# A fp32 decoder layer on TensorE: moving rows stored as even tokens, then odd tokens, and read from both halves in turns

## The reference

```
proj = rmsnorm(x) @ w_in          # q, k, v, r, a_lr, conv (3), chunk-MLP (2)
out  = concat[GLA(q,k,v,a), ShortConv, ChunkMLP] @ w_out
h    = x + out
y    = h + (silu(n @ w_gate) * (n @ w_up)) @ w_down,   n = rmsnorm(h), width 5632
y    = rmsnorm(y)
```

## Time and profile before

| | |
|---|---|
| median of 3 runs | 2201.98 us (2200.2 to 2202.89) |
| profiled execution, span from first to last instruction | 2202.0 us |
| instructions | 41269 |
| busy share of the span: TensorE, DVE, ACT | 99%, 78%, 46% |
| matmuls | 17357 |
| HBM read, written | 267.09 MB, 56.63 MB |

### The profile page before, as it was taken

One profiled execution on the slowest core, in us unless ns is written; L12 is line 12 of the kernel. 1 busy time (PEld: TensorE's weight loads), 2 busy tenths in 40 slices (PEclk: granted clock), 3 DMA queues, 4 the chain that ended last, 5 costly groups with the idle time before them and its releaser, 6 DMA issues.

```text
span 2202.0 us, 41269 instructions
## 1 busy us (share of the span) xinstructions
PE 2189.9 (99%) x17357; PEld 2181.0 (99%) x17357; DVE 1710.5 (78%) x1987; ACT 1002.5 (46%) x1331; POOL 9.6 (0%) x15
## 2 busy tenths in 40 slices
PE   9999999999999999999999999999999999999998
PEld 9999999999999999999999999999999999999998
DVE  7765378546796789888887887888888888787887
ACT  7433523224454554444444544444444545444455
POOL 0000000000000000000000000000000000000000
PEclk9999999999999999999999999999999999999998
DMA  5332224245333435445445445444545876555523
GB/s 189 96 107 85 96 72 148 81 126 188 127 105 103 156 104 170 128 143 164 140 132 165 140 131 155 153 129 141 165 140 166 301 280 223 183 205 190 187 81 117
DMA packets 121516, 325.51 MB, mean 148 GB/s; under 512 B 10699, under 2 KB 51211, under 8 KB 120364
## 3 DMA queue, kind: packets, MB, share of 16 engines
q1 hardware_dynamic: 120860, 323.69, 44.0%
q10 hardware_dynamic: 528, 0.07, 0.0%
HBM read 267.09 MB, written 56.63 MB: 147 GB/s over the span
## 4 chain that ended last, share of the span: by engine, by line
PE 93%; DVE 3%; issue 1%; ACT 1%; DMA 1%; POOL 0%; POOLq 0%; DVEq 0%; ACTq 0%; SPq 0%
PE acc L1613 36%; PE g L1613 27%; PE acc L1300 18%; PE acc L1524 2%; PE g L1524 2%; PE acc L1562 2%; PE g L1562 1%; PE acc L1516 1%; PE g L1516 1%; DMA w_raw<-w_in 1%; DVE w_lo L2178 0%; PE g L1327 0%; PE g L1450 0%; DVE kd L2040 0%; PE g L1457 0%
## 5 line engine op out<-in xcount | busy, mean ns | idle before, releaser
L1121 ACT CAST w_hi<-w_s 128x1024 fp32r<-128x1024 f32 (+1 forms) x204 | 209.6, 1027 | 358.6 <-DVE w_s L2407 350.7
L1613 PE MATMUL acc<-op_hi,w_hi 128*128 128x272 f32 x1056 | 305.8, 290 | 0.3 <-ACT acc L1095 0.3
L1613 PE MATMUL acc<-sg_hi,w_hi 128*128 128x272 f32 x1056 | 305.9, 290 | 0.0
L1613 PE MATMUL g<-op_hi,w_hi 128*128 128x272 f32 x1056 | 305.8, 290 | 0.0
L1613 PE MATMUL acc<-op_hi,w_lo 128*128 128x272 f32 x1056 | 305.6, 289 | 0.0
L1613 PE MATMUL g<-op_hi,w_lo 128*128 128x272 f32 x1056 | 305.6, 289 | 0.0
L1613 PE MATMUL acc<-sg_hi,w_lo 128*128 128x272 f32 x1056 | 305.6, 289 | 0.0
L1613 PE MATMUL acc<-sg_lo,w_hi 128*128 128x272 f32 x1056 | 304.0, 288 | 0.0
L1613 PE MATMUL g<-op_lo,w_hi 128*128 128x272 f32 x1056 | 304.0, 288 | 0.0
L1613 PE MATMUL acc<-op_lo,w_hi 128*128 128x272 f32 x1056 | 304.0, 288 | 0.0
L1300 PE MATMUL acc<-op_hi,w_hi 128*128 128x272 f32 x1280 | 269.3, 292 | 0.0
(11 more groups left out here) (390 smaller groups left out, 5004.0 us busy)
## 6 DMA issues: line engine op xcount, KB each, us to landing
w<-w_gu SPq DMA_DIRECT2D x88, 512.0 KB, 3.3
w_raw<-w_gu SPq DMA_DIRECT2D x88, 512.0 KB, 4.1
w_raw<-w_in SPq DMA_DIRECT2D x64, 512.0 KB, 3.5
hf_dram<-hf_hi SPq DMA_DIRECT2D x22, 952.0 KB, 6.6
hf_dram<-hf_lo SPq DMA_DIRECT2D x22, 952.0 KB, 8.8
w_raw<-w_d SPq DMA_DIRECT2D x32, 512.0 KB, 4.4
w<-w_d SPq DMA_DIRECT2D x26, 512.0 KB, 3.3
op_hi<-hf_dram SPq DMA_DIRECT2D x16, 544.0 KB, 7.0
```

The source lines that it names most:

```text
L1121: nc.scalar.copy(w_hi[:, (C_ST + n) % RING, 0:w], src[:, 0:w]).then_inc(hi_ready, 1)
L1613: last = nc.tensor.matmul(out, w, x, start=fresh and j == 0 and i == 0, stop=j == h - 1 and i == 2, skip_group_check=True)
```

## The change

Within each half of 272 tokens, every activation row that a projection moves is stored as 136 even tokens followed by 136 odd tokens. The matmul's moving access names 136 pairs, the inner step of a pair being 136 elements (544 bytes), so it reads token 0 from the first half, token 1 from the second, token 2 from the first, and so on. Tokens enter the array, and PSUM, in their natural order.

The input comes a second time, as `xP`, in the new order on the host side; `load_x` reads it, while the residual is loaded from `xT` as before. Passes that make rows out of PSUM results or natural-order tiles read every second element and write runs. `mix_single_hi` becomes three copies, one per form. `var1` sums squares of the permuted input, so it reads in turns too. The diff, cut to its core (the same edit of the matmul stands at L1327, L1516, L1524 and L1562):

```diff
+        def turns(ap):
+            return ap.rearrange("p (a b) -> p b a", a=2)
+        def pairs(ap):
+            return ap.rearrange("p (b a) -> p b a", a=2)
+        def split2(ap):
+            return ap.rearrange("p (h b a) -> p h a b", h=ap.shape[1] // TH, a=2)
+        def halves(ap):
+            return ap.rearrange("p (h a b) -> p h a b", h=ap.shape[1] // TH, a=2)
+        def split_rows(ap):
+            return ap.rearrange("p i (b a) -> p i a b", a=2)
+        def half_rows(ap):
+            return ap.rearrange("p i (a b) -> p i a b", a=2)
...
-                sp.dma_start(trunk[:, 2 * i:2 * i + 2, :], xT[:, 2 * i:2 * i + 2, :]).then_inc(x_in[i], 16)
+                sp.dma_start(trunk[:, 2 * i:2 * i + 2, :], xP[:, 2 * i:2 * i + 2, :]).then_inc(x_in[i], 16)
...
-                nc.scalar.copy(op_hi[:, k, :], mix[:, MIX_ORDER[k], :]).then_inc(op_h, 1)
+                nc.scalar.copy(halves(op_hi[:, k, :]), split2(mix[:, MIX_ORDER[k], :])).then_inc(op_h, 1)
...
-                nc.scalar.copy(fa_hi[:, 0], mg[:, :, 0, :])
-                nc.scalar.copy(fa_hi[:, 1:3], mg[:, :, 2:4, :].rearrange("p i b t -> p b i t")).then_inc(fa_h, 1)
+                for f, b in enumerate((0, 2, 3)):
+                    last = nc.scalar.copy(half_rows(fa_hi[:, f]), split_rows(mg[:, :, b, :]))
+                last.then_inc(fa_h, 1)
...
-                nc.scalar.copy(ta_hi[f], mg[:, :, T_OF[f], :]).then_inc(ta_h, 1)
+                nc.scalar.copy(half_rows(ta_hi[f]), split_rows(mg[:, :, T_OF[f], :])).then_inc(ta_h, 1)
...
-                nc.scalar.mul(trunk[:, m, :], hst[:, m % 4, :], vec[:, V_G2 + m:V_G2 + m + 1]).then_inc(xg_done, 1)
+                nc.scalar.mul(halves(trunk[:, m, :]), split2(hst[:, m % 4, :]), vec[:, V_G2 + m:V_G2 + m + 1]).then_inc(xg_done, 1)
...
-                        last = nc.tensor.matmul(acc[t % 2][:, a, 0:TH], w, x[:, k, a * TH:(a + 1) * TH],
+                        last = nc.tensor.matmul(pairs(acc[t % 2][:, a, 0:TH]), w, turns(x[:, k, a * TH:(a + 1) * TH]),
...
-                    last = ones_product(g01, rstd[:])
+                    last = ones_product(g01, rstd[:], turns, pairs)
...
-                            last = nc.tensor.matmul(out, w, x, start=fresh and j == 0 and i == 0,
+                            last = nc.tensor.matmul(pairs(out), w, turns(x), start=fresh and j == 0 and i == 0,
...
-                nc.vector.tensor_tensor(ta_lo[f], mg[:, :, T_OF[f], :], f32(ta_hi[f]), ALU.subtract).then_inc(ta_rdy, 1)
+                nc.vector.tensor_tensor(half_rows(ta_lo[f]), split_rows(mg[:, :, T_OF[f], :]), half_rows(f32(ta_hi[f])), ALU.subtract)\
+                    .then_inc(ta_rdy, 1)
...
-                nc.vector.tensor_tensor(op_lo[:, k, :], mix[:, MIX_ORDER[k], :], f32(op_hi[:, k, :]), ALU.subtract)\
+                nc.vector.tensor_tensor(halves(op_lo[:, k, :]), split2(mix[:, MIX_ORDER[k], :]), halves(f32(op_hi[:, k, :])), ALU.subtract)\
...
-                nc.vector.tensor_tensor(hid[:, 2 * (q % 2):2 * (q % 2) + 2, :], two(gate),
-                                        two(up), ALU.mult).then_inc(hid_done, 1)
+                nc.vector.tensor_tensor(half_rows(hid[:, 2 * (q % 2):2 * (q % 2) + 2, :]), split2(gate),
+                                        split2(up), ALU.mult).then_inc(hid_done, 1)
...
+        "xP": feature_major(x).reshape(P, KT, 2, TH // 2, 2).transpose(0, 1, 2, 4, 3).reshape(P, KT, T),
```

More of the change, by code:

```diff
@@ L136, in up, with build @@
         return self.n
-def build(nc, xT, w_alr, w_in, w_kv, w_kc, w_oa, w_out, w_gu, w_d4, w_d3, vecs, wa2, wm, wsbd, bs, s0, cbuf, ident, tri, maskA, maskS,
+def build(nc, xT, xP, w_alr, w_in, w_kv, w_kc, w_oa, w_out, w_gu, w_d4, w_d3, vecs, wa2, wm, wsbd, bs, s0, cbuf, ident, tri, maskA, maskS,
           bmask, yT, gla_p, gla_s, conv_o, cmv):
@@ L1326, in alr_products @@
                     for a in range(2):
-                        mm = nc.tensor.matmul(g23[:, a, 0:TH], alw[:, k, :], x[:, k, a * TH:(a + 1) * TH],
+                        mm = nc.tensor.matmul(pairs(g23[:, a, 0:TH]), alw[:, k, :], turns(x[:, k, a * TH:(a + 1) * TH]),
                                               start=(k == 0 and n == 0), stop=(k == KT - 1 and n == 1))
@@ L1344, in _, with ones_product @@
                     mm.then_inc(chunk_done, 1)
-            def ones_product(out2, buf):
+            def ones_product(out2, buf, order=lambda ap: ap, out_order=lambda ap: ap):
                 for a in range(2):
-                    last = nc.tensor.matmul(out2[:, a, 0:TH], onesf[:], buf[:, a * TH:(a + 1) * TH],
+                    last = nc.tensor.matmul(out_order(out2[:, a, 0:TH]), onesf[:], order(buf[:, a * TH:(a + 1) * TH]),
                                             start=True, stop=True)
@@ L1515, in kv_product @@
                             for i, (w, x) in enumerate(((w_h, x_h), (w_h, x_l), (w_l, x_h))):
-                                last = nc.tensor.matmul(bank[:, side, 0:TH], w, x, start=False,
+                                last = nc.tensor.matmul(pairs(bank[:, side, 0:TH]), w, turns(x), start=False,
                                                         stop=j == KT - 2 * HQ - 1 and i == 2, skip_group_check=True)
@@ L1523, in kv_product @@
                     for i, (w, x) in enumerate(((w_h, x_h), (w_h, x_l), (w_l, x_h))):
-                        last = nc.tensor.matmul(banks[idx][:, side, 0:TH], w, x, start=idx < 2 and j == 0 and i == 0,
+                        last = nc.tensor.matmul(pairs(banks[idx][:, side, 0:TH]), w, turns(x), start=idx < 2 and j == 0 and i == 0,
                                                 stop=j == HQ - 1 and i == 2, skip_group_check=True)
@@ L1561, in mix_product @@
                         for i, (w, x) in enumerate(((w_h, x_h), (w_h, x_l), (w_l, x_h))):
-                            last = nc.tensor.matmul(out, w, x, start=idx < 2 and j == 0 and i == 0,
+                            last = nc.tensor.matmul(pairs(out), w, turns(x), start=idx < 2 and j == 0 and i == 0,
                                                     stop=j == HP - 1 and i == 2, skip_group_check=True)
@@ L2201, in mix_forms @@
                 dve.wait_ge(fa_h, 1)
-                nc.vector.tensor_tensor(fa_lo[:, 0], mg[:, :, 0, :], f32(fa_hi[:, 0]), ALU.subtract)
+                nc.vector.tensor_tensor(half_rows(fa_lo[:, 0]), split_rows(mg[:, :, 0, :]), half_rows(f32(fa_hi[:, 0])), ALU.subtract)
                 for b in (1, 2):
-                    last = nc.vector.tensor_tensor(fa_lo[:, b], mg[:, :, b + 1, :], f32(fa_hi[:, b]), ALU.subtract)
+                    last = nc.vector.tensor_tensor(half_rows(fa_lo[:, b]), split_rows(mg[:, :, b + 1, :]), half_rows(f32(fa_hi[:, b])), ALU.subtract)
                 last.then_inc(fa_rdy, 1)
@@ L2683, in _ @@
             scale(0, pc, range(0, NV_OUT, 2))
-INS = ("xT", "w_alr", "w_in", "w_kv", "w_kc", "w_oa", "w_out", "w_gu", "w_d4", "w_d3", "vecs", "wa2", "wm", "wsbd", "bs", "s0", "cbuf",
+INS = ("xT", "xP", "w_alr", "w_in", "w_kv", "w_kc", "w_oa", "w_out", "w_gu", "w_d4", "w_d3", "vecs", "wa2", "wm", "wsbd", "bs", "s0", "cbuf",
        "ident", "tri", "maskA", "maskS", "bmask")
```

## The result

The changed kernel takes 2069.03 us (median of 4 runs, 2068.69 to 2072.32) against 2201.55 us (4 runs) for the kernel before: ratio 0.9401, 95% interval 0.9387 to 0.9414. The forecast was 2065 us, with 2025 to 2150 as the likeliest case's own range.

What follows compares the result with a forecast made beforehand. TensorE was taken to bound the kernel, by matmul count times spacing. 2202 - 137 (spacing) + 5 (missed handovers) = 2070, leaned down to 2065 us; range 2025 to 2440, the likeliest case 2025 to 2150.

Steps and rivals of the forecast that it cites:

- likeliest case: Whole kernel: a gain by the removed surplus in matmul spacing, DVE's limit included; 2025 to 2150 us, chance 0.57.
- What bounds the kernel: Whole kernel: nothing outside TensorE holds it; time is matmul count times spacing, 16,708 x 126 ns = 2,105 us.
- What 126 ns is made of: Matmul spacing: 115.6 ns for columns and fixed cost, plus 10.4 ns surplus in fetching the moving row from SBUF.
- Step 1: Moving access of the 16,708 matmuls: reading in pairs brings spacing to 117.8 ns, saving 8.2 ns each, 137 us.
- Step 2: DVE and ACT passes writing the new order: reading every second word adds zero; 58 us if it halved the rate.
- Step 3: Input loads as long as before; variance product on permuted squares costs nothing or a few hundred ns.
- Step 4: Block stages: faster TensorE asks sooner for weight forms, so a few handovers miss; 5 us added, 0 to 20.
- DVE takes over: Rival: surplus gone, but alternate-word passes cost twice and DVE sets the stages; 2,050 to 2,100 us, within the 0.57.
- Half rate: Rival on moving-row fetch: each fetch yields a single word, 229 ns a matmul, 3,920 us; chance 0.17.
- What would show it: Profile signs of being right: about 850 matmuls per 100 us, spacing 116 to 118 ns, no TensorE wait above 1 us.

Runs made afterwards that it cites:

- experiment 1: Separate kernel of matmuls alone, the layer left out: 48 back to back for each of 49 orders of reading; it ran in 523.4 us.
- experiment 5: Second separate kernel of matmuls alone, the layer left out: 48 in a row for each of 40 orders, varying steps and distances; it ran in 493.8 us.
- `half_of_lo`: Changed kernel with DVE subtracting only half of each `w_lo` block: 2046.06 us, ratio 0.929, beside 2201.23 us for the kernel before.
- `orders_alone`: The kernel of experiment 1: matmuls alone in 49 orders of reading, the layer left out; 523.4 us.
- `readers_and_lines`: The kernel of experiment 5: matmuls alone in 40 orders of reading, the layer left out; 493.8 us.

## Why the prediction was right, and where it was not

*What bounds the kernel* held: the time follows the spacing of matmuls, and the storage alone changes nothing.

*What 126 ns is made of* held within 0.2 ns: the surplus over 115.6 is in fetching the moving row and not in the weight load or a fixed cost, and 115.8 is what is left. Turning the order removes it entirely.

The Trainium skill ("TensorE: Matmul & The Clock Gate", back-to-back issue gap) gives 272/2.4 + 2.5 = 115.8 ns; before, the trace disagreed at 126, and now it agrees at 115.8 for this type too. (The 174 us that the prediction puts on this are 10.4 x 16,708; from the page's 115.8 it would be 10.2 x 16,708 = 170.)

*Step 1* had the right sign but the wrong size, and half of its reason was wrong. It took 8.2 ns a matmul, the middle between the surplus gone and the shortest spacing seen; the runs show 10.1 on the mean, 168 us for 137. The reason, neighbouring words colliding in one part of the memory with 544 bytes to spread them, fell with experiments 1 and 5: streams 1 or 2 elements apart are as fast. What stands is the other half of it, that each stream goes at half rate and then shows no surplus. The cause, as far as the runs carry it: a new line for each reader every 1.67 ns in order, against a price of 1.77 to 1.79. That the hardware has two such readers is a model, fitted on experiment 1. It met the new reduced-fp32 spacings of experiment 5 to within some 4 ns, readers by 5 (246.6 for 240) apart, and misses four streams; no record shows the readers themselves.

*Step 2*'s zero was right for DVE. ACT pays 16 x 72 + 8 x 59 + 4 x 123 ns = 2.1 us (L909: 702 against 643), and the three copies of `mix_single_hi` take 3.7 us for 3.1, in all where ACT has room. *Step 3*: the variance product on permuted squares has a mean of 465 ns against 392 for four matmuls, 0.3 us.

*Step 4* was too small: 32 us for 5, and outside its own 0 to 20. It named the right engine, DVE at 90.5% and 93% (measured 91.0 in 1600 to 1700, 91.8 in 1300 to 1400), but read the share of busy time as if the work were even. Gaps came where it is bunched: at the start, in 500 to 600, in 700 to 800 where the stages begin, at 1600 and at 2000. It also left out the loads, which DVE's progress releases and which now land late for ACT (81.4 us of waits between 800 and 1500). Of the 32 us, 21 go when DVE has half of its subtractions less. Of the other 11, 4 us stand at the start and 5 in 500 to 600 (in `half_of_lo` some 1.5 of these are a spell at the 1.2 GHz level, from 560.5 on); the waits there are for DVE's `w_lo` L1789, `op_lo` and `tmp`. They weren't taken apart further.

The two errors, 31 us too little gained and 27 too little given back, cancel. That the forecast of 2065 is within 4 us of the result is luck; its terms are not that good. *DVE takes over* was named as a rival inside the same range, for a reason that didn't hold (passes over alternate words cost nothing on DVE), but a fifth of the pace's gain did go to waits on DVE.

*Half rate* fell for this type. Others do pay for turns: bf16 rows take 258.7 ns in place of 115.8, more than double, and plain fp32 rows 287.7 in place of 229.2, a quarter more. The Trainium skill ("SBUF — State Buffer", box on cachelines), by which a line needs two consecutive hits, was the reason to give it a chance. Measured on rows read by a fixed step, what counts is how soon the next line is wanted; going back and forth between two lines has a price of its own (below) that no run here explains. For bf16 by 4, each line is hit twice and the row takes 241 ns, so two hits are not enough there; turns of the reduced fp32 type never hit a line twice in a row, and lose nothing.

*What would show it*: 850 matmuls per 100 us, found 866 where nothing waits; spacing 116 to 118, found 115.8; no wait above 1 us, found up to 2.0; the sign for a step 4 that is too small, waits of TensorE on DVE's `w_lo` (L2382 of before), came too.

Of the kernels that keep all of the work and the reference's order of tokens, the changed one is the fastest here. Mending the single gaps by reordering DVE's early and last passes was not tried.

## What to carry to other kernels

Before costing a new access order, measure the spacing of the same matmul alone, by type: the reading that saves 10 ns on a reduced-fp32 row of 272 costs 142 on a bf16 one. When the bounding engine is sped up by 9%, look at where its supplier's work is bunched and not at the supplier's mean share; 91% busy gave back a fifth of the gain. Look too at what the supplier releases: here loads of unchanged length came late because DVE asked for them late. Idle GpSimd is no free hand for work on SBUF beside a DVE near its limit.

## What the runs showed of the hardware that I had not expected

- A moving row pays per 16-byte line, about 1.77 ns for each new one: bf16 480.1 ns for 272 lines, plain fp32 by 4 480.7. This price doesn't follow TensorE's clock. In `orders_alone` and `readers_and_lines` the granted clock fell to its 1.2 GHz level while such rows ran (364.7 to 388.6 us and 425.0 to 462.5); bf16 by 6 took 361 ns on either side of the fall, and bf16 by 8 479.6 and 480.1. Of the plain fp32 row in order, in `orders_alone`, the first seven spacings, at that level, are 426 to 454 ns, and from the ninth on they are 229: a row that isn't held by its lines does follow the clock. The reduced fp32 type behaves as two readers with one such limit each (243.3 ns for 136 lines each).
- Going back to a line just left costs less than a new one, but not nothing: 258.7/272 = 0.95 ns for bf16 in turns, 1.06 for plain fp32; bf16 turns 4 elements apart take 172.5; a reduced fp32 row in four turns 145.0, which is 1.07 for each word of a reader. No run here explains that size.
- Weights loaded from every second, third and fourth word, with the row in turns: 117.7, 173.4 and 233.3 ns. For the fourth word the row in order has the same 233.4, so the load of weights sets the spacing there.
- bf16 matmuls of 256 columns written to every second PSUM column take 214.9 ns, against 109.6 for neighbours.
- A DVE pass with both operands in SBUF that begins beside a GpSimd pass ends as if begun at about its end (2.90 us for 0.72, 42 passes); one with an operand in PSUM isn't held (0.44 us beside it, 0.43 else, 22 passes each).
